# A two-layer trunk on one core: the first head unit begun on 256 tokens, and layer 1's first weights prepared between the chunks of h

## The chip, the cores and the metric

The kernel runs on one NeuronCore of a Trainium2 chip. The engines are TensorE (PE, with its weight loads shown apart as PEld), VectorE (DVE), ScalarE (ACT), GpSimd (POOL) and SyncE (SP), each with its own instruction queue; they meet only at semaphores. The metric is the device time of one execution in microseconds (us).

## The reference, cut to what matters

Two layers over 512 tokens of width 1024. Layer 0 has sliding attention with sinks, layer 1 has differential attention; each is followed by a gated feed-forward block of width 2816 with a three-tap convolution.

```python
def rms_norm(x, gain):
    y = xf * lax.rsqrt(jnp.mean(xf * xf, axis=-1, keepdims=True) + NORM_EPS)
    return (y * gain).astype(x.dtype)
...
for i in range(DEPTH):                      # DEPTH = 2
    h = rms_norm(x, attn_norm[i])
    y = sliding_sink_attention(h, ...) if kind == 0 else differential_attention(h, ...)
    x = x + y
    x = x + conv_ffn(rms_norm(x, ffn_norm[i]), ffn_w_up[i], ffn_conv_w[i], ffn_conv_b[i], ffn_w_down[i])
return rms_norm(x, final_norm)
...
q, k, v = split(h @ w_in)                   # q and k then turned by cos and sin of the positions
a = silu(conv(h @ w_up_a) + conv_b) * (h @ w_up_gate);  y = a @ w_down
```

## The kernel before

Every float32 product is made of three passes on TensorE in a 32-bit format of reduced precision: an operand is split in a high part (`w_hi`, `h_hi`, a rounded copy that ScalarE makes) and a low part (`w_lo`, `h_lo`, the difference, which VectorE makes; GpSimd made it for the first two weight blocks). So a weight block goes by DMA to `raw`, by ScalarE to `w_hi`, by VectorE to `w_lo`, and only then may TensorE use it. `raw`, `w_hi` and `w_lo` have two slots of 3072 columns. Blocks of the attention are cut in four parts of 768 columns (two chunks of 128 input features each); blocks of the down projection fill only the first 1024 columns of a slot, which are parts 0 and 1 of what follows in it.

The activations `xT` (features on partitions, tokens along the row) are eight chunks `kc` of 128 features x 512 tokens. `h = xT * gain` is split chunk by chunk: ScalarE writes `h_hi` (L1031), VectorE `h_lo` (L1383). The factor of the mean square is applied later, when a projection's tile is taken out of PSUM (`take`, L1055 to L1060).

**The start.** SP issues the loads in order: positions, the first gain, the four 128-token tiles of x (512 KB each), the first weight block in two halves of three DMAs, the second block, the small vectors. TensorE turns x with 32 transposes (L545), tile by tile. VectorE works out the angles of the rotation, copies each chunk from PSUM (L1504) and subtracts (L1383); ScalarE takes the four sines, the squares of two tiles, and then alternates between `h_hi` and a part of `w_hi`. GpSimd subtracts the eight parts of the first two blocks (L518). TensorE's first projection (L594) is the head unit 0: two token tiles side by side chunk by chunk (48 products of 384 columns), then the other two tiles (48 more), then the first tile of unit 1 (24), then the head transposes of unit 0 (L608). These need the rotated q and k: `take` of all four tiles by ScalarE, then `rope` on VectorE (L1395 to L1400), and the vectors copied by `little_vectors` (L1512 to L1519).

**The end of the down projection of layer 0.** The last pair of blocks is ordered so that the eight output chunks end one after the other: with 16 groups of three products, chunks 0 to 3 end with groups 4, 6, 8 and 10, chunks 4 to 7 with groups 12 to 15 (counted from 0). VectorE adds each to `xT` (L1628) and subtracts for `h_lo`; ScalarE writes `h_hi`. The first unit of layer 1 needs the parts of its weight block in slot 0: parts 2 and 3 can be split as soon as they have landed, parts 0 and 1 only when block 20 of the down projection has been read, which is after group 11. The semaphore `lo_done` counts parts in the order 2, 3, 0, 1. TensorE's first product there waits for part 0, that is for the third count, and for chunk 0 of `h_lo`. The program order of ScalarE and VectorE is written out by hand in each engine's block.

## Time and profile before

| | us |
|---|---|
| median of three runs | 1174.99 (1174.76 to 1175.63) |
| the profiled execution, its own time | 1174.54 |
| its span in the trace | 1172.8 |
| TensorE busy | 1140.1 (97%) |
| VectorE busy | 688.9 (59%) |
| ScalarE busy | 462.2 (39%) |
| GpSimd busy | 19.0 (2%) |

The trace covers 1172.8 us of the 1174.54; the other 1.7 us lie around it. In the timeline, an instruction's listed time reaches some 0.08 us into the next one's on VectorE and ScalarE, and about 0.16 us on TensorE for 384 columns, since instructions are pipelined. What an engine needs per instruction is the distance between two starts.

### The profile page before, as it was taken

The page shows a single profiled execution, that of the slowest core. Times are in us where ns is not written, and L with a number is a line of the kernel's source. Part 1 is how long each engine was busy: PE and PEld are TensorE (multiplying, and loading weights), DVE is VectorE, ACT ScalarE, POOL GpSimd, SP SyncE. Part 2 cuts the span into 40 slices and gives each one's busy share as a digit, 9 for nine tenths or more (in the row PEclk, how much of TensorE's full clock was granted, in tenths as well). Part 3 has the DMA queues.
Part 4 walks back from the last instruction along what each step waited for, and adds up shares of the span by engine and source line. Part 5 has one row for each costly group of instructions (what it writes and reads, how often), then busy time and mean ns, then how long its engine had stood idle before and what let it go on. Part 6 is the DMA issues. An engine that isn't in the chain of part 4 may idle for free.

```text
span 1172.8 us, 15982 instructions
## 1 busy us (share of the span) xinstructions
PE 1140.1 (97%) x5752; PEld 966.2 (82%) x5752; DVE 688.9 (59%) x1153; ACT 462.2 (39%) x939; POOL 19.0 (2%) x36
## 2 busy tenths in 40 slices
PE   7999899999999999998999999999999999999997
PEld 6998688888888878887999988778888888888886
DVE  5588765565565553337577777855556556553334
ACT  6577653122122222336455556554212212222324
POOL 4100000000000000000000000000000000000000
PEclk8999999999999999999999999999999999999999
DMA  7211223323323222325112311214332332213222
GB/s 225 72 37 37 73 88 92 96 84 107 105 74 107 72 72 94 102 89 162 55 54 69 94 36 36 72 40 122 108 92 86 107 103 76 89 54 105 92 91 106
DMA packets 146603, 101.94 MB, mean 87 GB/s; under 512 B 12073, under 2 KB 139270, under 8 KB 146566
## 3 DMA queue, kind: packets, MB, share of 16 engines
q1 hardware_dynamic: 146566, 101.45, 28.1%
q8 instruction: 23, 0.38, 0.1%
q14 instruction: 14, 0.11, 0.0%
HBM read 99.34 MB, written 2.10 MB: 86 GB/s over the span
## 4 chain that ended last, share of the span: by engine, by line
PE 87%; DVE 7%; ACT 4%; issue 1%; DMA 1%; SPq 0%; DVEq 0%; ACTq 0%
PE ps L529 22%; PE ps L531 22%; PE ps L530 21%; PE ps L594 15%; PE ps L608 2%; PE ps L746 2%; ACT prob L1091 1%; DVE w_lo L1354 1%; DVE h_lo L1383 1%; PE ps L772 1%; PE ps L818 1%; DVE ot_lo L1563 1%; ACT w_hi L1014 1%; ACT prob L1101 1%; DVE den L1441 0%
## 5 line engine op out<-in xcount | busy, mean ns | idle before, releaser
L1014 ACT ACTIVATE w_hi<-raw 128x512 fp32r<-128x512 f32 (+2 forms) x212 | 192.5, 940 | 302.6 <-PE ps L531 299.7
L529 PE MATMUL ps<-h_hi,w_lo 128*128 128x512 f32 x704 | 274.7, 390 | 0.0
L531 PE MATMUL ps<-h_hi,w_hi 128*128 128x512 f32 x704 | 273.9, 389 | 0.0
L530 PE MATMUL ps<-h_lo,w_hi 128*128 128x512 f32 x704 | 273.9, 389 | 0.0
L1354 DVE TENSOR_TENSOR w_lo<-raw,w_hi 128x512 fp32r<-128x512 f32 (+2 forms) x204 | 215.6, 1082 | 6.2 <-ACT w_hi L1014 6.2
L530 PEld LDWEIGHTS ps<-h_lo,w_hi 128*128 128x128 f32 x704 | 132.1, 188 | 27.9 <-issue 0.5
L529 PEld LDWEIGHTS ps<-h_hi,w_lo 128*128 128x128 f32 x704 | 132.1, 188 | 27.7 <-issue 0.5
L531 PEld LDWEIGHTS ps<-h_hi,w_hi 128*128 128x128 f32 x704 | 132.1, 188 | 27.6
L594 PE MATMUL ps<-w_hi,h_lo 128*128 128x384 f32 x384 | 133.4, 347 | 8.6 <-DVE w_lo L1354 4.5
L594 PE MATMUL ps<-w_hi,h_hi 128*128 128x384 f32 x384 | 133.2, 347 | 0.0
L594 PE MATMUL ps<-w_lo,h_hi 128*128 128x384 f32 x384 | 132.5, 345 | 0.0
L1657 DVE TENSOR_TENSOR normed<-ps,rstd 128x512 f32<-128x512 f32 x44 | 30.4, 692 | 173.1 <-PE ps L531 160.3
L1648 DVE TENSOR_TENSOR u_lo<-u_all,u_hi 128x512 fp32r<-128x512 f32 x44 | 30.4, 692 | 139.9 <-ACT u_hi L1216 139.9
L1216 ACT ACTIVATE u_hi<-u_all 128x512 fp32r (+1 forms) x44 | 27.7, 630 | 149.6 <-PE ps L531 149.6
L594 PEld LDWEIGHTS ps<-w_hi,h_lo 128*128 128x128 f32 x384 | 73.6, 192 | 13.0 <-issue 5.6
L594 PEld LDWEIGHTS ps<-w_lo,h_hi 128*128 128x128 f32 x384 | 73.5, 191 | 0.7
L594 PEld LDWEIGHTS ps<-w_hi,h_hi 128*128 128x128 f32 x384 | 73.4, 191 | 0.4
L529 PE MATMUL ps<-u_hi,w_lo 128*128 128x512 f32 x176 | 68.7, 390 | 0.6 <-DVE u_all L1666 0.3
L529 PE MATMUL ps<-w_hi,u_lo 128*128 128x512 f32 x176 | 68.8, 391 | 0.2 <-DVE w_lo L1354 0.2
L531 PE MATMUL ps<-u_hi,w_hi 128*128 128x512 f32 x176 | 68.5, 389 | 0.0
L530 PE MATMUL ps<-u_lo,w_hi 128*128 128x512 f32 x176 | 68.5, 389 | 0.0
L531 PE MATMUL ps<-w_hi,u_hi 128*128 128x512 f32 x176 | 68.5, 389 | 0.0
(188 smaller groups left out, 1583.2 us busy)
## 6 DMA issues: line engine op xcount, KB each, us to landing
raw<-in_ffn_w_up SPq DMA_DIRECT2D x88, 512.0 KB, 4.5
raw<-in_ffn_w_down SPq DMA_DIRECT2D x44, 512.0 KB, 3.3
raw<-in_b_w_in SPq DMA_DIRECT2D x24, 512.0 KB, 4.9
raw<-in_a_w_out SPq DMA_DIRECT2D x4, 1024.0 KB, 4.9
raw<-in_b_w_out SPq DMA_DIRECT2D x4, 1024.0 KB, 4.7
raw<-in_a_w_in SPq DMA_DIRECT2D x3, 1024.0 KB, 5.8
x_tok<-in_x SPq DMA_DIRECT2D x4, 512.0 KB, 4.8
out<-x_tok SPq DMA_DIRECT2D x8, 256.0 KB, 2.0
```

What stands on the lines that cost most here:

```text
L529: pe.matmul(out_, a_lo, b_hi, start=start, stop=False)
L530: pe.matmul(out_, a_hi, b_lo, start=False, stop=False)
L531: return pe.matmul(out_, a_hi, b_hi, start=False, stop=stop)
L594: ins = pe.matmul(ps[:, pj(u, t), 0:UW], a[:, kc, tok], b[:, kc, :], start=(kc == 0 and m == 0), stop=(kc == KC - 1 and m == 2))
L608: ins = pe.transpose(ps[:, bank, c * P:(c + 1) * P], i, ident[:, :])
L746: pe.matmul(ps[:, s_bank(t) + e, 0:n], a[rows, 0, q], b[rows, 1, 0:n], start=(m == 0), stop=False)
L772: ins = pe.matmul(both, v[:, s, k, :], pt[:, :, k * P:(k + 1) * P], start=(i == 0), stop=(i == len(passes) - 1))
L1014: act.activation(w_hi[:, s, at], raw[:, s, at], ACT.Copy).then_inc(hi_done, 1)
L1216: act.activation(u_hi[:, s, :], u_all[:, bass.ds(f, 1), :], ACT.Copy).then_inc(uhi_done, 1)
L1354: dve.tensor_tensor(w_lo[:, s, at], raw[:, s, at], w_hi[:, s, at].bitcast(F32), ALU.subtract).then_inc(lo_done, 1)
L1648: dve.tensor_tensor(u_lo[:, s, :], u_all[:, bass.ds(f, 1), :].rearrange("p a b -> p (a b)"), u_hi[:, s, :].bitcast(F32), ALU.subtract).the ...
L1657: own.link(dve.tensor_tensor(a, ps[:, 2 * s, :], rstd[:, :], ALU.mult))
```

## The change

At the start:

- SP loads two tiles of x, both halves of the first weight block, and then the other two tiles. The positions and the gain are loaded from ScalarE's queue. ScalarE loads the table with the sines at once and the other one later.
- TensorE runs 12 transposes of the identity that nobody reads (`keep_running`), then turns two tiles, then 32 more unread transposes, then the new `first_pair`: the projection of tiles 0 and 1, and after each of its chunks 3 to 6 four transposes of tiles 2 and 3. The projection of tiles 2 and 3 then goes chunk by chunk over both.
- Copies, `h_hi` and `h_lo` of unit 0's h are made in halves of 256 tokens.
- GpSimd subtracts no weights. VectorE subtracts the first block's parts between the halves of h, and the second block's after two tiles of v.
- The angles, the squares and the sines come after the first half of h and the first block's weights.

At the end of layer 0's down projection, ScalarE makes a part of `w_hi` after each of the first four chunks of `h_hi`, in the order 2, 3, 0, 1, where parts 2 and 3 came ahead of all chunks and 0 and 1 after the fourth and fifth. VectorE subtracts a part after each of the chunks 0 to 3 of `h_lo`, where 2 and 3 came ahead of all of its additions and 0 and 1 after chunks 4 and 5.

```diff
-            for t in range(NT):
+            for t in range(2):
                 sp.dma_start(x_tok[:, t, :], xv[:, t, :]).then_inc(x_landed[t], 16)
...
+            for t in range(2, NT):
+                sp.dma_start(x_tok[:, t, :], xv[:, t, :]).then_inc(x_landed[t], 16)
...
+            def keep_running(k):
+
+
+                for _ in range(k):
+                    pe.transpose(ps[:, 3, 0:P], ident[:, :], ident[:, :])
+
+            keep_running(12)
...
+            for t in range(2):
                 pe.wait_ge(x_landed[t], 16)
...
+                    ins = pe.transpose(first_x(kc, t), x_tok[:, t, kc * P:(kc + 1) * P], ident[:, :])
+                    if t == 1:
+                        ins.then_inc(x_tr0, 1)
+            keep_running(32)
...
+            def first_pair():
+
+
+                wh = w_hi[:, 0, :].rearrange("p (k n) -> p k n", k=KC)
+                wl = w_lo[:, 0, :].rearrange("p (k n) -> p k n", k=KC)
+                pe.wait_ge(posT_done, 2)
+                for kc in range(KC):
+                    if kc % 2 == 0:
+                        pe.wait_ge(lo_done, part_done("attnA", 0, kc // 2))
+                    pe.wait_ge(hlo_done0, kc + 1)
+                    for t in range(2):
+                        tok = slice(t * P, (t + 1) * P)
+                        ins = hi_lo(ps[:, t, 0:UW], h_hi[:, kc, tok], h_lo[:, kc, tok],
+                                    wh[:, kc, :], wl[:, kc, :], start=(kc == 0), stop=(kc == KC - 1))
+                        if kc == KC - 1:
+                            ins.then_inc(proj_done, 1)
+                    if kc >= FIRST_BACK:
+                        for t in range(2, NT):
+                            pe.wait_ge(x_landed[t], 16)
+                        for k in (2 * (kc - FIRST_BACK), 2 * (kc - FIRST_BACK) + 1):
+                            if k >= KC:
+                                continue
+                            pe.wait_ge(x_ready0, k // 2 * 2 + 2)
+                            for t in range(2, NT):
+                                ins = pe.transpose(first_x(k, t), x_tok[:, t, k * P:(k + 1) * P], ident[:, :])
+                            ins.then_inc(x_tr, 1)
...
+            act.dma_start(pos_i[:, :], positions.rearrange("b (t p) -> (b t) p", p=P))\
+               .then_inc(pos_landed, 16)
+            act.dma_start(grow[:, :], attn_norm[0].rearrange("(k p) -> k p", p=P))\
+               .then_inc(gain_landed, 16)
+            act.preload_act_table_set("trig_and_small")
...
+            for kc in range(0, KC, 2):
+                gained0(0, kc)
+                gained0(0, kc + 1)
+                high0(kc // 2)
+            for t in range(NT):
+                square_tokens(t)
+            trigonometry()
+            for kc in range(4):
+                gained0(1, kc)
+            act.preload_act_table_set("natural_log_exp_and_others")
             act.wait_ge(const_done, CONSTS)
             act.wait_ge(x_sq, NT)
             rsqrt(NORM["A"], rstd_tok[:, :], x_ss[:, :], 1.0 / D)
-
-
-            high("attnA", 1, 0, None, 0)
-            for t in range(NT):
+            for kc in range(4, KC):
+                gained0(1, kc)
+                if kc % 2:
+                    take("A", 0, 0, kc // 2 - 2)
+            for c in range(4):
+                high("attnA", 1, 0, None, c, wait=(c == 0))
+            for t in range(2, NT):
                 take("A", 0, 0, t)
-                if t < NT - 1:
...
-                high("attnB", 0, 0, None, 2, wait=True)
-                high("attnB", 0, 0, None, 3)
                 for dc in range(KC):
                     gained(NORM["B"], dc, vecT[:, 1, R_ATTN + dc:R_ATTN + dc + 1])
-                    if 3 <= dc < 5:
-                        high("attnB", 0, 0, (down, FB - 2), dc - 3, wait=False)
+                    if dc < 2:
+                        high("attnB", 0, 0, None, 2 + dc, wait=(dc == 0))
+                    elif dc < 4:
+                        high("attnB", 0, 0, (down, FB - 2), dc - 2, wait=False)
...
+            for kc in range(4):
+                copy_x(0, kc)
+            for kc in range(0, KC, 2):
+                low_h0(0, kc)
+                low_h0(0, kc + 1)
+                low_w("attnA", 0, 0, kc // 2)
+                if kc < 4:
+                    copy_x(0, kc + 4)
+                    copy_x(0, kc + 5)
+            angles()
+            copy_x(1, 0)
+            copy_x(1, 1)
+            for kc in range(KC):
+                low_h0(1, kc)
+                if kc + 2 < KC:
+                    copy_x(1, kc + 2)
...
+                    for c in range(4 if kind == "A" and t == 1 else 0):
+                        low_w("attnA", 1, 1, c)
...
-                    if 5 <= dc < 7:
-                        low_w("attnB", 0, 0, dc - 5)
+                    if 1 <= dc < 5:
+                        low_w("attnB", 0, 0, (dc + 1) % 4)
 
                 if l == 0:
-                    low_w("attnB", 0, 0, 2)
-                    low_w("attnB", 0, 0, 3)
```

TensorE at the start of the program, before (`x_tok` holds x by token tiles, `ps` is PSUM; `lo_done` counts weight parts, `hlo_done` chunks of h):

```order
L545 MATMUL ps<-ident,x_tok 128x128 [waits x_landed0]
L545 MATMUL ps<-ident,x_tok 128x128 x5
L545 MATMUL ps<-ident,x_tok 128x128 [waits posT_done]
L545 MATMUL ps<-ident,x_tok 128x128
L545 MATMUL ps<-ident,x_tok 128x128 [waits x_landed1]
L545 MATMUL ps<-ident,x_tok 128x128 x7
L545 MATMUL ps<-ident,x_tok 128x128 [waits x_landed2]
L545 MATMUL ps<-ident,x_tok 128x128 x7
L545 MATMUL ps<-ident,x_tok 128x128 [waits x_landed3]
L545 MATMUL ps<-ident,x_tok 128x128 x7
L594 MATMUL ps<-w_hi,h_lo 128x384 [waits hlo_done,lo_done,const_done]
```

and in the changed kernel:

```order
L538 MATMUL ps<-ident 128x128 [waits ident_done]
L538 MATMUL ps<-ident 128x128 x11
L542 MATMUL ps<-ident,pos_f 128x4 [waits pos_done]
L544 MATMUL ps<-ident,grow 128x8 [waits gain_landed]
L549 MATMUL ps<-ident,x_tok 128x128 [waits x_landed0]
L549 MATMUL ps<-ident,x_tok 128x128 x7
L549 MATMUL ps<-ident,x_tok 128x128 [waits x_landed1]
L549 MATMUL ps<-ident,x_tok 128x128 x7
L538 MATMUL ps<-ident 128x128 x32
L528 MATMUL ps<-w_hi,h_lo 128x384 [waits lo_done,hlo_done0,posT_done,const_done]
L529 MATMUL ps<-w_lo,h_hi 128x384
L530 MATMUL ps<-w_hi,h_hi 128x384
```

The first projection moved from behind four tiles' transposes to behind those of two and 44 unread ones.

VectorE at the end of layer 0's down projection, before:

```order
L1354 TENSOR_TENSOR w_lo<-raw,w_hi 128x768 [waits hi_done] x2
L1628 TENSOR_TENSOR xT<-xT,ps 128x512 [waits down_done] x2
L1383 SCALAR_TENSOR_TENSOR h_lo<-xT,vecs,h_hi 128x512 [waits hhi_done]
L1628 TENSOR_TENSOR xT<-xT,ps 128x512 [waits down_done]
L1383 SCALAR_TENSOR_TENSOR h_lo<-xT,vecs,h_hi 128x512 [waits hhi_done]
L1628 TENSOR_TENSOR xT<-xT,ps 128x512 [waits down_done]
L1383 SCALAR_TENSOR_TENSOR h_lo<-xT,vecs,h_hi 128x512 [waits hhi_done]
L1628 TENSOR_TENSOR xT<-xT,ps 128x512 [waits down_done]
L1383 SCALAR_TENSOR_TENSOR h_lo<-xT,vecs,h_hi 128x512 [waits hhi_done]
L1628 TENSOR_TENSOR xT<-xT,ps 128x512 [waits down_done]
L1383 SCALAR_TENSOR_TENSOR h_lo<-xT,vecs,h_hi 128x512 [waits hhi_done]
L1354 TENSOR_TENSOR w_lo<-raw,w_hi 128x768 [waits hi_done]
```

and in the changed kernel:

```order
L1712 TENSOR_TENSOR xT<-xT,ps 128x512 [waits down_done] x2
L1441 SCALAR_TENSOR_TENSOR h_lo<-xT,vecs,h_hi 128x512 [waits hhi_done]
L1412 TENSOR_TENSOR w_lo<-raw,w_hi 128x768 [waits hi_done]
L1712 TENSOR_TENSOR xT<-xT,ps 128x512 [waits down_done]
L1441 SCALAR_TENSOR_TENSOR h_lo<-xT,vecs,h_hi 128x512 [waits hhi_done]
L1412 TENSOR_TENSOR w_lo<-raw,w_hi 128x768 [waits hi_done]
L1712 TENSOR_TENSOR xT<-xT,ps 128x512 [waits down_done]
L1441 SCALAR_TENSOR_TENSOR h_lo<-xT,vecs,h_hi 128x512 [waits hhi_done]
L1412 TENSOR_TENSOR w_lo<-raw,w_hi 128x768 [waits hi_done]
L1712 TENSOR_TENSOR xT<-xT,ps 128x512 [waits down_done]
L1441 SCALAR_TENSOR_TENSOR h_lo<-xT,vecs,h_hi 128x512 [waits hhi_done]
L1412 TENSOR_TENSOR w_lo<-raw,w_hi 128x768 [waits hi_done]
```

The first additions moved ahead of the first two weight parts, and the last two parts moved up among chunks 2 and 3.

ScalarE at the same place, before:

```order
L1014 ACTIVATE w_hi<-raw 128x768 [waits raw_landed0]
L1014 ACTIVATE w_hi<-raw 128x768
L1031 ACTIVATE h_hi<-xT,vecs 128x512 [waits x_ready] x4
L1014 ACTIVATE w_hi<-raw 128x768 [waits down_used]
L1031 ACTIVATE h_hi<-xT,vecs 128x512 [waits x_ready]
L1014 ACTIVATE w_hi<-raw 128x768
L1031 ACTIVATE h_hi<-xT,vecs 128x512 [waits x_ready] x3
```

and in the changed kernel:

```order
L1067 ACTIVATE h_hi<-xT,vecs 128x512 [waits x_ready]
L1050 ACTIVATE w_hi<-raw 128x768 [waits raw_landed0]
L1067 ACTIVATE h_hi<-xT,vecs 128x512 [waits x_ready]
L1050 ACTIVATE w_hi<-raw 128x768
L1067 ACTIVATE h_hi<-xT,vecs 128x512 [waits x_ready]
L1050 ACTIVATE w_hi<-raw 128x768 [waits down_used]
L1067 ACTIVATE h_hi<-xT,vecs 128x512 [waits x_ready]
L1050 ACTIVATE w_hi<-raw 128x768
L1067 ACTIVATE h_hi<-xT,vecs 128x512 [waits x_ready] x4
```

Each part of `w_hi` now follows a chunk of `h_hi`; the wait for the landed block stands behind the first chunk.

## Rows read from the trace of the kernel before

**Rows 1.** The page, part 1: engine, busy us (share), instructions.
```profile
PE 1140.1 (97%) x5752; PEld 966.2 (82%) x5752; DVE 688.9 (59%) x1153; ACT 462.2 (39%) x939; POOL 19.0 (2%) x36
```

**Rows 2.** To 19.4 us: length, busy PE, PEld, DVE, ACT, POOL; PEclk; DMA share; GB/s.
```profile
4.80:10.80 6.00, 5.91 (x32) 5.68 (x32) 1.24 (x6) 4.17 (x9) 0.00 (x0) 1.00 1.06 364
10.80:14.40 3.60, 0.00 (x0) 0.01 (x1) 3.60 (x5) 3.57 (x6) 1.96 (x2) 0.78 1.13 356
14.40:19.40 5.00, 4.98 (x16) 5.00 (x17) 5.00 (x6) 3.25 (x5) 5.00 (x3) 0.50 0.83 227
```

**Rows 3.** Waits of 0 to 48 us: total, times, longest us.
```profile
PE ps L594 <- POOL w_lo L518: 3.7, 1, 3.7
```

**Rows 4.** Groups of instructions, 8 to 28 us: busy us, mean ns, idle before.
```profile
L518 POOL TENSOR_TENSOR w_lo<-raw,w_hi 128x768 fp32r<-128x768 f32 x5 | 10.5, 2116 | 13.8 <-ACT w_hi L1014 13.8
L1383 DVE SCALAR_TENSOR_TENSOR h_lo<-xT,vecs,h_hi 128x512 fp32r<-128x512 f32 x8 | 9.7, 1229 | 0.0
...
L1031 ACT ACTIVATE h_hi<-xT,vecs 128x512 fp32r<-128x512 f32 x8 | 5.7, 715 | 5.0 <-DVE xT L1504 5.0
L1504 DVE COPY xT<-ps 128x512 f32<-128x512 f32 x8 | 5.3, 681 | 4.7 <-PE ps L545 4.7
L1014 ACT ACTIVATE w_hi<-raw 128x768 fp32r<-128x768 f32 x6 | 5.0, 832 | 0.0
...
L1119 ACT ACTIVATE sq<-x_tok 128x1024 f32<-128x1024 f32 x4 | 4.2, 1055 | 0.2
```

**Rows 5.** TensorE at the end of the first down projection.
```profile
540.10 0.39 PE L531 MATMUL ps<-u_hi,w_hi 128*128 128x512 f32 x1
544.97 0.45 PE L594 MATMUL ps<-w_hi,h_lo 128*128 128x384 f32 x1 [4.48 <-DVE w_lo L1354]
```

**Rows 6.** VectorE there.
```profile
535.03 1.83 DVE L1354 TENSOR_TENSOR w_lo<-raw,w_hi 128x768 fp32r<-128x768 f32 x2 [2.55 <-ACT w_hi L1014]
536.78 1.28 DVE L1628 TENSOR_TENSOR xT<-xT,ps 128x512 f32<-128x512 f32 x2
...
543.97 0.95 DVE L1354 TENSOR_TENSOR w_lo<-raw,w_hi 128x768 fp32r<-128x768 f32 x1
```

**Rows 7.** ScalarE there.
```profile
534.16 1.58 ACT L1014 ACTIVATE w_hi<-raw 128x768 fp32r<-128x768 f32 x2 [2.67 <-DMA raw<-in_b_w_in]
...
557.13 1.28 ACT L1252 ACT_TABLE_LOAD   x1
```

**Rows 8.** Busy time by stretch at that place, columns as in rows 2.
```profile
545.00:550.00 5.00, 5.00 (x20) 5.00 (x21) 4.77 (x8) 2.94 (x5) 0.00 (x0) 0.66 0.29 84
```

**Rows 9.** The chain that ended last, from 540 us.
```profile
544.97 15.71 PE ps L594 x80
...
561.47 7.04 PE ps L594 x40
```

**Rows 10.** The same helper where GpSimd is quiet, 527 to 549 us, columns as in rows 4.
```profile
L1383 DVE SCALAR_TENSOR_TENSOR h_lo<-xT,vecs,h_hi 128x512 fp32r<-128x512 f32 x8 | 6.0, 746 | 0.3 <-ACT h_hi L1031 0.2
```

**Rows 11.** DMA issues begun near 3.35 us: KB, us from issue to landing.
```profile
x_tok<-in_x SPq DMA_DIRECT2D x1, 512.0 KB, 6.2
raw<-in_a_w_in SPq DMA_DIRECT2D x1, 512.0 KB, 7.0
```

**Rows 12.** Weight loads of the x transposes, first 4.8 to 8.3 us.
```profile
L545 PEld LDWEIGHTS ps<-ident,x_tok 128*128 128x128 f32 x17 | 3.5, 224 | 1.9 <-DMA x_tok<-in_x 1.9
```

**Rows 13.** The same weight loads, 9 to 11 us.
```profile
L545 PEld LDWEIGHTS ps<-ident,x_tok 128*128 128x128 f32 x12 | 1.6, 156 | 0.0
```

**Rows 14.** TensorE, the first head transposes after the first unit.
```profile
38.87 1.47 PE L608 MATMUL ps<-ident,qk 128*128 128x128 f32 x12
```

**Rows 15.** VectorE, the last step before those transposes.
```profile
3.82 0.64 DVE L1490 SCALAR_TENSOR_TENSOR ang<-turns,ang 128x32 f32<-128x32 f32 x3
...
37.98 0.36 DVE L1519 TENSOR_SCALAR nsink<-sink_in 64x16 f32<-64x16 f32 x2
```

**Rows 16.** ScalarE, end of the first head unit: start us, us.
```profile
34.69 0.31 ACT L1055 ACTIVATE qk<-ps,vecs 128x64 f32<-128x64 f32 x1 [2.44 <-PE ps L594]
```

More of the change, by code:

```diff
@@ L44 @@
 UA, UB = 4, 8
+FIRST_BACK = 3
 OB, ODC = 4, 2
@@ L66 @@
 CONSTS = 1 + HALF + 4 + 10
-FIRST_LOWS = 2
 ALU = mybir.AluOpType
@@ L510, in _ @@
             pool.wait_ge(const_done, CONSTS)
-            def low(ph, s, i):
-                n = cols(ph) // parts(ph)
-                for c in range(parts(ph)):
-                    at = slice(c * n, (c + 1) * n)
-                    pool.wait_ge(hi_done, part_done(ph, i, c))
-                    pool.tensor_tensor(w_lo[:, s, at], raw[:, s, at], w_hi[:, s, at].bitcast(F32),
-                                       ALU.subtract).then_inc(lo_done, 1)
-            for i in range(FIRST_LOWS):
-                low("attnA", i, i)
         @block.tensor
@@ L622, in start_unit0 @@
             def start_unit0(kind):
-                slabs = chain(projection(kind, 0, 0, (0, 1)), projection(kind, 0, 0, (2, 3)))
-                run(slabs, 12 + 8)
+                if kind == "A":
+                    first_pair()
+                    slabs = projection(kind, 0, 0, (2, 3))
+                    run(slabs, 8)
+                else:
+                    slabs = chain(projection(kind, 0, 0, (0, 1)), projection(kind, 0, 0, (2, 3)))
+                    run(slabs, 12 + 8)
                 if kind == "B":
@@ L1120, in square_tokens, with gained0, high0 @@
                                accum_out=x_ss[:, t:t + 1]).then_inc(x_sq, 1)
-            square_tokens(0)
-            square_tokens(1)
-            for kc in range(KC):
-                gained(NORM["A"], kc, vecT[:, 0, R_ATTN + kc:R_ATTN + kc + 1])
-                if kc == 0:
-                    act.wait_ge(half_landed, 16 * 3)
-                if kc < 4:
-                    high("attnA", 0, 0, None, kc, wait=(kc == 2))
-            square_tokens(2)
-            square_tokens(3)
+            def gained0(pair, kc):
+                act.wait_ge(x_ready if pair else x_ready0, kc + 1)
+                at = pair_cols(pair)
+                act.activation(h_hi[:, kc, at], xT[:, kc, at], ACT.Copy,
+                               scale=vecT[:, 0, R_ATTN + kc:R_ATTN + kc + 1])\
+                   .then_inc(hhi_done if pair else hhi_done0, 1)
+            def high0(c):
+                if c == 0:
+                    act.wait_ge(half_landed, 16 * 3)
+                high("attnA", 0, 0, None, c, wait=(c == 2))
+            for kc in range(0, KC, 2):
[8 more added lines that the diff above has]
+            act.preload_act_table_set("natural_log_exp_and_others")
             act.wait_ge(const_done, CONSTS)
@@ new lines, in copy_x, with low_h0 @@
+            def copy_x(pair, kc):
+                dve.wait_ge(x_tr if pair else x_tr0, kc // 2 * 2 + 2)
+                dve.tensor_copy(xT[:, kc, pair_cols(pair)], first_x(kc)).then_inc(x_ready if pair else x_ready0, 1)
+            def low_h0(pair, kc):
+                dve.wait_ge(hhi_done if pair else hhi_done0, kc + 1)
+                at = pair_cols(pair)
+                dve.scalar_tensor_tensor(out=h_lo[:, kc, at], in0=xT[:, kc, at],
+                                         scalar=vecT[:, 0, R_ATTN + kc:R_ATTN + kc + 1],
+                                         in1=h_hi[:, kc, at].bitcast(F32), op0=ALU.mult,
+                                         op1=ALU.subtract).then_inc(hlo_done if pair else hlo_done0, 1)
```

84 lines of the change are left out of this document (38 added, 46 removed).

## The prediction

> **What bounds the kernel now.** The page comes first: TensorE is busy for 97% of the span [rows 1], so only its gaps and its slow stretches can be won, and the change touches two. The stretches of the start show 3.6 us without a product between the last transpose of x and the first product, and behind them 5.0 us with 16 products at granted clock 0.50, the 1.2 GHz level [rows 2]. The waits name what ended that gap: the first low part of the weights, from GpSimd [rows 3]. The groups say why all this is slow: GpSimd needs 2,116 ns for a part, and VectorE's `h_lo`, which reads two SBUF tensors, has a mean of 1,229 ns beside it [rows 4], while copies of the same size from PSUM take 681 ns [rows 4]. The second place is the end of layer 0's down projection. TensorE starts its last product there at 540.10 and the next at 544.97, waiting 4.48 us for a low part on VectorE [rows 5]. VectorE did not make its first addition until 536.78, because two weight parts stood ahead of it and were waiting for a transfer that ended at 534.16 [rows 6, 7]. The granted clock then is 0.66 over 545 to 550 us [rows 8], and the first 80 products take 15.71 us, where 40 others take 7.04, or 0.175 each [rows 9].
>
> **Durations used.** Start to start, VectorE's instruction is about 0.08 us shorter than listed (two additions in 1.28, each listed near 0.68 [rows 6]); likewise on ScalarE. For 256 columns there is no row. Bounds are half of the 512-column pitch and the whole of it: 0.30 to 0.60 for a copy, 0.33 to 0.66 for `h_lo` (its pitch is 0.66, from 746 ns where GpSimd is quiet [rows 10]), 0.31 to 0.63 for `h_hi` [rows 4]. I take 0.34, 0.39 and 0.42, near the half, since 768 columns against 512 on ScalarE cost 832 against 715 ns [rows 4], which leaves a fixed part of some 0.2 to 0.4. A weight part costs ScalarE 0.75 and VectorE 0.87 [rows 4, 6].
>
> **The start, part by part.**
>
> *Loads.* Positions and gain leave SP's queue, so x starts about 0.8 us sooner; a tile of x needs 1.4 us of the transfer engines (the first had landed at 4.85, the fourth, issued near 2.9, 6.2 later [rows 2, 11]). Two tiles then land at about 4.1 and 5.3. The first weight half landed at 10.4 to 11.4 [rows 11]; with two tiles fewer ahead I put it at 7.7. The second half follows at 10.5, and tiles 2 and 3, now behind both, at 13.8 instead of 9.1. The second block and the small vectors are needed later than they land.
>
> *TensorE up to the first product.* The weight loads of the x transposes took 224 ns at first and 156 on average from 9 us on [rows 12, 13], although the granted clock reads 1.00 all through [rows 2]: the engine began at 1.2 GHz and rose after some 4.5 us of transposes alone. Twelve unread transposes from 1.5 us cost 2.5 us at that level. They cover nothing but the wait for x (4.1), so they cost at most 0.2. If the clock rises 4.5 us after that, at 6.0, the transposes of x end at 7.0 and the 32 unread ones (0.11 each, as in rows 14, where twelve take some 1.3) at 10.5. The page "TensorE: Matmul & The Clock Gate" of the Trainium skill, section "Part 4: PE-mode transpose", says that full clock "doesn't engage" for transposes, which do not count as busy in the same way. By that rule the unread transposes would only delay; rows 12 and 13 contradict it here, and it is the second rival below.
>
> *The first weights.* VectorE copies four halves of chunks from 6.6 on; ScalarE has two `h_hi` at 7.9 and `w_hi` at 8.6; VectorE has the two `h_lo` by then and the part at 9.6. That is before the unread transposes end, so the first product starts at 10.5, against 14.42 before (where rows 2 change). The later parts come at 11.9, 14.2 and 15.9, and TensorE needs them at 12.6, 15.1 and 18.1: nothing waits. The first pair is 48 products at 0.175 plus 16 transposes at 0.11, together 10.2 us, to 20.7.
>
> *The second pair.* VectorE does the angles (ten small operations at 0.21 [rows 15], 2.1 us) and two copies until 18.8. ScalarE is later: four squares at 1.24 from 14.0 to 19.0 (1,055 ns [rows 4] and a read of the sum), sines 0.5, then `h_hi`. Its first chunk of the second half is ready at 20.5, just under TensorE's 20.7. ScalarE then loads a table (1.28 [rows 7]) and makes the reciprocal root, done at 23.9; chunk 4 is ready at 24.9 and TensorE wants it at 24.9. So 48 products end at 29.2.
>
> *The chain behind it.* TensorE adds 24 products and two transposes of vectors and would reach the head transposes at 33.8. ScalarE does not let it: from 23.9, four `h_hi` (1.7), two takes at 0.95, four parts of the second block (3.0), so takes 2 and 3 begin at 30.5, and the last one at 31.4. Before, from the last take's start to the head transposes' inputs it was 34.69 to 38.3 at most [rows 15, 16], of which 3.4 is work. So they start at 31.4 + 3.4 + latency = 34.9. Before they started at 38.87 [rows 14]. **Gain 3.9 us**, and TensorE idles about 1.1 us at that point, which is what is late next. GpSimd's parts and the slow `h_lo` go at no cost: VectorE has 8 x 0.87 more, and its idle time above covers it.
>
> **The end of the down projection.** TensorE's groups last 0.68 us (three products) and the last begins its third product at 540.10 [rows 5]. So chunk 0 is done at 533.0, chunks 1 to 3 at 534.4, 535.7 and 537.1, and block 20 has been read at 537.8. VectorE was free from 532.5. In the new order VectorE adds chunk 0 at 533.0 and ScalarE has `h_hi` 0 at 534.4, when the transfer has just ended [rows 7]. Then the two engines alternate: additions 0.60, `h_lo` 0.66, parts 0.87 on VectorE. Part 2 is done at 536.6, part 3 at 538.7, part 0 (its `w_hi` started at 537.9, just after block 20 was read) at 540.9, part 1 at 543.0. Before, part 0 started at 543.97 [rows 6]. The first product comes at 540.9 instead of 544.97: 4.05 us. TensorE reaches chunk 2 at 543.0, when part 1 is there; every later chunk (2.13 us of VectorE for two at 1.26, against 2.1 on TensorE) is ready before it. With a gap of 0.6 us the clock stays up: 80 products take 14.0 instead of 15.71, 1.7 more.
>
> What could eat it: the squares' end moves only 1.6 us forward, and four parts and the table load follow. The load started at 557.13 [rows 7]; it now starts at 555.6 and ends at 556.9, where the mean square is there at 555.7. The takes are thus 1.3 us late against a slack of 1.6 before the head transposes, and unit 1's first product waits perhaps 0.1. **Gain 5.7 us.**
>
> **Sum.** 3.9 + 5.7 = 9.6 us. Against the profiled execution's own 1174.54 that is 1164.9; the median of the runs lies 0.45 above that execution, so I predict **1165.4 us**. The stretches in between are a stream on TensorE that is not touched.
>
> **Rivals.**
>
> 1. *Two helpers too slow at the start.* If halves cost nearer their upper bound, some 20% more on VectorE, the schedule above ends at 37.8 instead of 34.9. For: both queues have many short waits on each other, and small instructions have fixed costs. Against: rows 4 and 6. Time: 1.1 + 5.7 gained, 1168.2.
> 2. *Transposes don't hold the clock.* TensorE stays at 1.2 GHz: the 32 unread ones then take 7 us and the first product starts at 14.5, with the clock rising some 5 us later. Head transposes at 40.0, 1.1 late. Only the second place gains: 1174.99 + 1.1 - 5.7 = 1170.4. Against it stand rows 12 and 13.
> 3. *The second place gains only in part*, say because the weight transfer lands later or the clock falls all the same: 2.2 us less, 1167.6.
> 4. *Slower.* The transfer of x tiles 2 and 3 is the mechanism: the first pair's chunk 3 is followed by a wait for both, in TensorE's own order, with the rest of the first pair queued behind. From a landing at 15.2 on each microsecond costs one; the start stops winning at 20.2 and the whole kernel loses from about 25.9. At 28 it would be 1177. Against: 2.6 MB stand ahead, at 356 to 364 GB/s [rows 2] some 7 us.
> 5. *It does nothing*, because TensorE's later waits give both gains back: 1175.
>
> **Chances.** Forecast 60%, rival 1 17%, rival 3 10%, rival 2 8%, rival 4 2%, rival 5 3%. Lower bound: no lateness of ScalarE (33.8, 5.1 gained), first product a little sooner and 5.8 at the second place, or 1163.3. The upper end takes in rivals 1 and 3: 1168.6. About 0.2% (2.35 us) is what a measurement of this kernel can tell from no change. Forecast and rivals 1 to 3 lie beyond that: faster 95%, same 3%, slower 2%.
>
> **What would show it.** Right: the first projection product near 10.5 us at full clock; no GpSimd work after 5 us; the head transposes near 34.9, released by VectorE; no gap above 1 us before layer 1's first product (near 537, since all there comes 3.9 sooner) and no half clock after it. Wrong: a clock of 0.50 between 10 and 20 us; a wait of TensorE for x tiles; a wait for the low part at the second place over 1.5 us.

## The result and the profile after

| | before | after |
|---|---|---|
| median of the runs, us | 1175.05 (1174.76 to 1175.63) | 1165.69 (1165.55 to 1165.93) |
| span of the profiled execution, us | 1172.8 | 1163.7 |

The ratio is 0.9918, with a 95% interval of 0.9904 to 0.9932. The changed kernel is 9.4 us faster; the prediction was 1165.4 us, in a range from 1163.3 to 1168.6. Timed once more (e8 below) it was 10.7 us faster by the medians, mostly because the kernel before was slower there (1175.8). The two ratios have overlapping intervals, and the account below, which follows one trace of each kernel, explains 9.1 us.

The page of the changed kernel, part 1 (engine, busy us, share, instructions), answers to [rows 1]:

```profile
PE 1141.4 (98%) x5796; PEld 966.4 (83%) x5796; DVE 693.7 (60%) x1177; ACT 464.8 (40%) x947; POOL 3.0 (0%) x28
```

TensorE has 44 instructions more (the unread transposes) and the span is 9.1 us shorter. GpSimd has lost 16 us of work, VectorE has gained only 4.8 us of busy time although it took over eight weight parts: its own `h_lo` became faster.

**The start, TensorE.** The timeline of the changed kernel (start us, length us, line, operation, tiles, count, idle time and its releaser):

```profile
1.53 2.82 PE L538 MATMUL ps<-ident 128*128 128x128 f32 x12 [1.53 <-POOL ident L505]
...
4.59 2.85 PE L549 MATMUL ps<-ident,x_tok 128*128 128x128 f32 x16
7.28 3.66 PE L538 MATMUL ps<-ident 128*128 128x128 f32 x32
10.72 0.41 PE L528 MATMUL ps<-w_hi,h_lo 128*128 128x384 f32 x1
```

The first product starts at 10.72, without a wait, where it started at 14.42 before. Products then follow each other by 0.175 us; before, the first 16 took 5 us at granted clock 0.50 [rows 2]. The window of 10 to 15 us, which answers to [rows 2], is full at granted clock 1.00 (columns: length; busy us of PE, PEld, DVE, ACT, POOL; PEclk; DMA share; GB/s):

```profile
10.00:15.00 5.00, 5.00 (x33) 4.89 (x32) 5.00 (x11) 4.40 (x9) 0.00 (x0) 1.00 1.04 382
```

**The start, the helpers.** Groups of instructions over the first 28 us (busy us, mean ns, idle before) and two rows of the timelines, which answer to [rows 4]:

```profile
L1170 ACT ACTIVATE h_hi<-xT,vecs 128x256 fp32r<-128x256 f32 x16 | 7.4, 503 | 5.7 <-DVE xT L1564 5.7
L1569 DVE SCALAR_TENSOR_TENSOR h_lo<-xT,vecs,h_hi 128x256 fp32r<-128x256 f32 x16 | 7.3, 480 | 2.5 <-ACT h_hi L1170 2.4
```

```profile
6.90 1.42 DVE L1564 COPY xT<-ps 128x256 f32<-128x256 f32 x4 [2.03 <-PE ps L549]
...
8.62 0.85 ACT L1050 ACTIVATE w_hi<-raw 128x768 fp32r<-128x768 f32 x1 [0.35 <-DMA raw<-in_a_w_in]
```

**The head transposes.** They start at 35.00 instead of 38.87 [rows 14], behind VectorE, and this is now the only wait that the view of waits lists for TensorE between 5 and 40 us (total us, times, longest us):

```profile
PE ps L639 <- DVE vecs L1597: 0.7, 1, 0.7
```

**The end of the down projection.** TensorE's last product there and the first of layer 1 answer to [rows 5]:

```profile
536.40 0.39 PE L530 MATMUL ps<-u_hi,w_hi 128*128 128x512 f32 x1
537.23 0.44 PE L598 MATMUL ps<-w_hi,h_lo 128*128 128x384 f32 x1 [0.45 <-DVE w_lo L1412]
```

From start to start that is 0.83 us instead of 4.87. The chain of work that ended last, from there on, answers to [rows 9]:

```profile
534.18 0.87 DVE w_lo L1412
535.05 0.60 DVE xT L1712
535.65 0.66 DVE h_lo L1441
536.31 0.88 DVE w_lo L1412
537.19 0.04 issue
537.23 14.19 PE ps L598 x80
551.42 0.79 PE ps L571 x8
552.20 7.15 PE ps L598 x40
559.35 0.87 PE ps L639 x8
```

The 80 products take 14.19 us instead of 15.71. Ahead of them the chain runs over VectorE alone (addition, `h_lo`, low part, 2.13 us a round): VectorE still ends last there, by under half a microsecond.

**Where 9.1 us went.** 3.87 at the head transposes; 0.17 of it is lost again up to the last product of the down projection (536.40 against 540.10, or 3.70); 4.04 in the gap; 1.52 in the 80 products; minus 0.11 in the next 40. That makes 9.15 us at layer 1's head transposes (559.35 against 568.51 in the chain before), and the span is 9.1 shorter.

### The profile page after: what moved, and what is told of

The parts are those of the page before. It is cut to its first block, busy times and chain, and to the rows that moved or that the text cites. A ratio compares the mean times of both kernels' runs of the same rounds, so it can differ in the third digit from the quotient of the medians.

```text
span 1163.7 us, 16099 instructions
## 1 busy us (share of the span) xinstructions
PE 1141.4 (98%) x5796; PEld 966.4 (83%) x5796; DVE 693.7 (60%) x1177; ACT 464.8 (40%) x947; POOL 3.0 (0%) x28
## 4 chain that ended last, share of the span: by engine, by line
PE 87%; DVE 6%; ACT 5%; issue 1%; DMA 1%; SPq 0%; DVEq 0%; ACTq 0%
PE ps L528 22%; PE ps L530 22%; PE ps L529 22%; PE ps L598 14%; PE ps L639 2%; PE ps L782 2%; ACT prob L1127 1%; DVE w_lo L1412 1%; PE ps L808 1%; ACT w_hi L1050 1%; PE ps L854 1%; DVE ot_lo L1648 1%; DMA raw<-in_a_w_in 1%; ACT prob L1137 1%; DVE den L1499 0%
## 5 line engine op out<-in xcount | busy, mean ns | idle before, releaser
L1412 DVE TENSOR_TENSOR w_lo<-raw,w_hi 128x512 fp32r<-128x512 f32 (+2 forms) x212 | 223.1, 1077 | 4.4 <-ACT w_hi L1050 4.4
L598 PE MATMUL ps<-w_hi,h_lo 128*128 128x384 f32 x368 | 126.5, 344 | 0.4 <-DVE w_lo L1412 0.4
L598 PE MATMUL ps<-w_hi,h_hi 128*128 128x384 f32 x368 | 126.2, 343 | 0.0
L598 PE MATMUL ps<-w_lo,h_hi 128*128 128x384 f32 x368 | 125.5, 341 | 0.0
L598 PEld LDWEIGHTS ps<-w_hi,h_lo 128*128 128x128 f32 x368 | 69.2, 188 | 5.0 <-issue 2.1
L598 PEld LDWEIGHTS ps<-w_lo,h_hi 128*128 128x128 f32 x368 | 69.2, 188 | 0.7
L598 PEld LDWEIGHTS ps<-w_hi,h_hi 128*128 128x128 f32 x368 | 69.2, 188 | 0.4
L529 PE MATMUL ps<-w_lo,u_hi 128*128 128x512 f32 x176 | 68.5, 389 | 0.0
```

Source lines behind the costliest of these rows:

```text
L529: pe.matmul(out_, a_hi, b_lo, start=False, stop=False)
L598: ins = pe.matmul(ps[:, pj(u, t), 0:UW], a[:, kc, tok], b[:, kc, :], start=(kc == 0 and m == 0), stop=(kc == KC - 1 and m == 2))
L1412: dve.tensor_tensor(w_lo[:, s, at], raw[:, s, at], w_hi[:, s, at].bitcast(F32), ALU.subtract).then_inc(lo_done, 1)
```

## Experiments

The theory: two gains that add, one at each place. At the start it is the first product that comes earlier and at full clock, and the head transposes are then held up by ScalarE's chain and not by TensorE. GpSimd's parts are slow themselves and slow VectorE down. At the second place, the order on VectorE and ScalarE. The rivals are those of the prediction. "Head" below is the start of the first head transposes, "layer 1" the start of its first product, both from the profile. Every kernel was timed beside the kernel before, whose median was 1176.05 next to e1 to e4, 1175.8 next to e5 to e8 and 1175.66 next to e9 and e10.

| kernel | head | layer 1 | median us | ratio, 95% interval |
|---|---|---|---|---|
| before | 38.87 | 544.97 | 1175.05 | |
| changed | 35.00 | 537.23 | 1165.69 | 0.9918 (0.9904 to 0.9932) |
| e8, changed again | 34.51 | 536.68 | 1165.12 | 0.9910 (0.9896 to 0.9923) |
| e1, second place alone | 39.45 | 542.11 | 1169.9 | 0.9946 (0.9933 to 0.9960) |
| e2, start alone | 34.31 | 540.50 | 1170.12 | 0.9954 (0.9941 to 0.9968) |
| e3, no unread transposes | 35.59 | 537.65 | 1165.4 | 0.9910 (0.9895 to 0.9925) |
| e4, before with 38 unread | 38.81 | 545.13 | 1173.58 | 0.9981 (0.9972 to 0.9990) |
| e5, early angles | 35.29 | 537.30 | 1164.92 | 0.9904 (0.9889 to 0.9919) |
| e6, e5 without unread | 35.66 | 538.24 | 1164.52 | 0.9902 (0.9887 to 0.9917) |
| e7, GpSimd's parts back | 38.23 | 540.34 | 1169.25 | 0.9942 (0.9929 to 0.9956) |
| e9, e5 with 22 unread | 33.91 | 536.00 | 1164.15 | 0.9901 (0.9887 to 0.9915) |
| e10, x tiles 2 and 3 late | 38.72 | 541.24 | 1168.75 | 0.9939 (0.9926 to 0.9952) |

In the kernels with the new second place, layer 1 starts 502.0 to 502.7 us after the head transposes, whatever happened ahead of them: what is won or lost at the start arrives there within 0.7 us.

e8 is the changed kernel, unedited, beside e5 to e7. It was expected 9.4 us under the kernel before, with the head transposes at 35.0 and a ratio within 0.3 us of the first one. It came 10.7 us under by the medians, with the head transposes at 34.51 and a ratio that is 0.9 us lower, so comparisons of two kernels to within 1 us need their traces too.

### e1 and e2: each place alone

e1 is the kernel before with only this:

```diff
-                high("attnB", 0, 0, None, 2, wait=True)
-                high("attnB", 0, 0, None, 3)
...
-                    if 3 <= dc < 5:
-                        high("attnB", 0, 0, (down, FB - 2), dc - 3, wait=False)
+                    if dc < 2:
+                        high("attnB", 0, 0, None, 2 + dc, wait=(dc == 0))
+                    elif dc < 4:
+                        high("attnB", 0, 0, (down, FB - 2), dc - 2, wait=False)
...
-                    if 5 <= dc < 7:
-                        low_w("attnB", 0, 0, dc - 5)
+                    if 1 <= dc < 5:
+                        low_w("attnB", 0, 0, (dc + 1) % 4)
...
-                    low_w("attnB", 0, 0, 2)
-                    low_w("attnB", 0, 0, 3)
```

> The kernel before with only the second edit: at the end of layer 0's down projection, ScalarE's and VectorE's weight parts between the chunks of h. My theory (the two places add, and the second is worth 4.0 us of gap and 1.5 us of clock): 5.5 us less than before, 1169.5 us, ratio 0.9953. Rival (the gain of the changed kernel comes from the start, and the second gap would come back later): less than 2 us.

e2 is the changed kernel with these lines undone.

> The changed kernel with the second edit undone, so only the start is new. My theory: 3.7 to 3.9 us less than before, 1171.2 us, ratio 0.9967; with e1 the two gains add up to that of both. Rival (an overlap between the two): the gains of e1 and e2 add up to more or less than the whole by over 1 us.

Measured: 1169.9 and 1170.12 against 1176.05, or 6.2 and 5.9 us less by the medians (5.4 by the ratio of e2). Both are more than expected: 5.5 for e1, 3.7 to 3.9 for e2. The chain of e1 shows the whole gain of the second place without the start:

```profile
542.06 0.04 issue
542.11 14.19 PE ps L594 x80
556.29 0.79 PE ps L567 x8
557.08 7.16 PE ps L594 x40
```

The chain of e2 shows the old second place under the new start:

```profile
540.50 15.71 PE ps L598 x80
556.21 0.79 PE ps L571 x8
556.99 7.04 PE ps L598 x40
```

The spans are 4.4 and 4.5 us shorter than before; in e1 the untouched start came 0.58 later than in the trace of before (39.45), so its own part is 5.0. 5.0 and 4.5 make 9.5, where both together gave 9.1: by the traces the gains add within 0.4 us. The medians alone don't show it: they add up to 12.1 against 9.4 for the changed kernel and 10.7 for e8. That is over the 1 us that the rival asked for, but each ratio is known only to about 1.6 us. What stands is that in e1 the 80 products and the gap before them are those of the changed kernel (14.19, and 0.84 from 541.27), and that in e2 they are those of the kernel before (15.71, and 4.87 from 535.63).

### e3: without the unread transposes

```diff
-            keep_running(12)
...
-            keep_running(32)
```

> The changed kernel without any of the 44 unread transposes. Theory A (they hold the clock, and ScalarE's chain hides most of that): the first products run at half clock for 2 to 5 us, but the head transposes wait for ScalarE and VectorE anyway, so 0 to 0.7 us more than the changed kernel. Theory B (the clock is what wins the start): 2 to 3 us more. The Trainium skill's page TensorE: Matmul & The Clock Gate, Part 4, says transposes do not count as busy; by it nothing would change in the clock, and the first product would start no later than now.

Measured: 1165.4, ratio 0.9910, the same as the changed kernel in e8. The clock does fall. TensorE in e3:

```profile
4.67 3.29 PE L548 MATMUL ps<-ident,x_tok 128*128 128x128 f32 x16
11.25 0.66 PE L528 MATMUL ps<-w_hi,h_lo 128*128 128x384 f32 x1 [3.29 <-DVE w_lo L1410]
11.71 0.52 PE L529 MATMUL ps<-w_lo,h_hi 128*128 128x384 f32 x1
...
14.44 0.34 PE L529 MATMUL ps<-w_lo,h_hi 128*128 128x384 f32 x1
...
35.59 1.47 PE L637 MATMUL ps<-ident,qk 128*128 128x128 f32 x12
```

Nine products cost 0.32 instead of 0.175 until 14.26, and the granted clock of 10 to 15 us is 0.66. That makes 1.3 us, and 0.5 more for a first product at 11.25. But the head transposes come only 0.59 later than in the changed kernel and wait for nobody: ScalarE's lateness had covered the rest. The account closes. From the first product to the head transposes TensorE needs 22.98 and 23.00 us in e5 and e9 below, where it neither waits nor slows down; it takes 24.28 in the changed kernel and 24.19 in e8, so the helpers hold it up by 1.2 to 1.3 us there, and 24.34 in e3, where the slow products fill the same 1.3 us. Without the unread transposes the clock fell, so the last sentence of the expectation did not come true.

### e4: unread transposes in the gap of the kernel before

```diff
+                if kind == "B":
+                    pe.wait_ge(x_ready, KC * NORM["B"] + 1)
+                    for _ in range(38):
+                        pe.transpose(ps[:, 0, 0:P], ident[:, :], ident[:, :])
```

> The kernel before with nothing but 38 unread transposes of the identity (about 4.2 us at full clock) put into the 4.5 us gap ahead of layer 1's first product. If transposes hold the clock, the granted clock stays 1.00 over 545 to 550 us and the first 80 products take 14.1 us instead of 15.71: 1.5 us less than before, 1173.5 us. If transposes do not count, the clock falls as before and the time is that of before, within 0.3 us.

Measured: 1173.58, ratio 0.9981 (0.9972 to 0.9990), so 1.2 to 3.3 us less; the expected 1.5 lies within, and the spans differ by 1.4. TensorE at that place, the piece of the chain, and the window that answers to [rows 8] (same columns, granted clock 1.00 for 0.66):

```profile
540.32 4.31 PE L628 MATMUL ps<-ident 128*128 128x128 f32 x38
545.13 0.45 PE L594 MATMUL ps<-w_hi,h_lo 128*128 128x384 f32 x1 [0.50 <-DVE w_lo L1358]
```

```profile
545.13 14.20 PE ps L594 x80
```

```profile
545.00:550.00 5.00, 4.87 (x28) 4.80 (x29) 4.77 (x9) 2.77 (x5) 0.00 (x0) 1.00 0.27 78
```

The gap before the product is as long as before, but it is filled with transposes, and the 80 products take 14.20 instead of 15.71 [rows 9]. So transposes alone keep the engine at 2.4 GHz. The page "TensorE: Matmul & The Clock Gate" of the Trainium skill, section "Part 4: PE-mode transpose", says the full clock doesn't engage for transpose mode, next to figures for bf16; for the float32 transposes of this kernel these rows contradict that. The run also splits the second place's gain: 1.5 us are the clock and the other 4.0 the gap itself.

### e5, e6 and e9: the helpers' work put into their idle time

In the changed kernel ScalarE waits 4.4 us for the first copy of x, while it later works out four squares and the sines in a row. e5 puts the angles, the first two squares and the sines there:

```diff
+            square_tokens(0)
+            square_tokens(1)
+            trigonometry()
             for kc in range(0, KC, 2):
...
-            for t in range(NT):
+            for t in range(2, NT):
                 square_tokens(t)
-            trigonometry()
...
+            angles()
             for kc in range(4):
                 copy_x(0, kc)
```

> The changed kernel with its ScalarE and VectorE work for the start put into the idle time before the first h_hi: VectorE works out the ten small steps of the angles from 4.8 us, ahead of the copies of x, and ScalarE squares tiles 0 and 1 and makes the sines ahead of the first h_hi. Nothing is left out. Theory A (the helpers' chain, not TensorE, sets when the head transposes start in the changed kernel, 35.00 against 34.0 at which TensorE is ready): ScalarE's work behind the first pair shrinks by 3 us, the takes of tiles 2 and 3 start with the end of their products near 29.7, head transposes at 34.2, total 0.8 us under the changed kernel of the same call. Rival B: the first h_hi moves from 7.36 to 8.5 or later because the square of tile 1 has to wait for its tile, the first product comes 0.5 to 1 us later, and nothing is gained: within 0.3 us of the changed kernel.

e6 is e5 without the 12 and 32 unread transposes.

> The kernel of e5_early_angles without the 12 and the 32 unread transposes, nothing else. Theory A (the unread transposes are worth about 1.6 us on TensorE, which in the changed kernel lies under ScalarE's lateness): with the helpers early nothing hides the slow products any more; the first nine or ten products run at the 1.2 GHz pitch of 0.32, head transposes near 35.6 and total 1.4 us above e5. Rival B (what e3 showed holds whatever the helpers do): within 0.4 us of e5.

Measured: 1164.92 and 1164.52, so e5 is 0.2 us under e8 and e6 0.4 under e5. In both the size is that of rival B and not that of theory A, but mostly for another reason than rival B's. ScalarE was early enough (the take of tile 2 begins after 2.0 us of idle time at 30.59 in e5; in e8 it begins at 30.20 straight behind the weight parts), but TensorE was later. TensorE in e5:

```profile
5.05 3.68 PE L549 MATMUL ps<-ident,x_tok 128*128 128x128 f32 x16
...
12.31 0.42 PE L528 MATMUL ps<-w_hi,h_lo 128*128 128x384 f32 x1
...
35.29 1.47 PE L639 MATMUL ps<-ident,qk 128*128 128x128 f32 x12
```

All 16 transposes of x ran at the 1.2 GHz pace (0.22 each), so the 32 unread ones ended at 12.3, when VectorE's low part had been there since 10.9. In e6 it is the products that pay:

```profile
11.10 0.41 PE L528 MATMUL ps<-w_hi,h_lo 128*128 128x384 f32 x1 [2.99 <-DVE w_lo L1412]
...
12.25 0.52 PE L528 MATMUL ps<-w_hi,h_lo 128*128 128x384 f32 x1
...
15.71 0.34 PE L530 MATMUL ps<-w_hi,h_hi 128*128 128x384 f32 x1
```

The window of 12 to 16 us of e6 has granted clock 0.57, that of 11 to 12 still 1.00:

```profile
12.00:16.00 4.00, 4.00 (x16) 4.00 (x15) 4.00 (x9) 3.39 (x6) 0.00 (x0) 0.57 1.06 357
```

The clock falls at 12.2, although the first product found it high, and 11 products cost 0.315: 1.5 us. In e5 the unread transposes cost 1.4 us of waiting for their own end. The two kernels differ by 0.4 us in total time, which their runs don't tell apart. The profiled execution of e6 was its slowest (1166.35, the others 1164.47 to 1164.57), so the slow products need not be in the others.

The explanation was that 32 are too many for an engine that is at 1.2 GHz when they begin. e9 has 22:

```diff
-            keep_running(32)
+            keep_running(22)
```

> The kernel of e5_early_angles with 22 instead of 32 unread transposes behind those of x, nothing else. In e5 the first low part was ready at 10.9 and TensorE reached the first product only at 12.31, because the transposes ran at the 1.2 GHz pitch until about 9.3 us. Theory A (the length of the row of unread transposes sets the first product there, and its clock is kept by a gap under 0.5 us): first product 11.1 to 11.5 at 0.17 to 0.18 pitch, head transposes at 34.4, which no helper holds up, total 0.9 us under e5, so 0.9896 of the kernel before. Rival B (with fewer of them the clock falls for part of the first pair, as in e6): 9 or more products at the 0.32 pitch, head transposes at 35.3 to 35.8, total within 0.5 us of e5.

Measured: 1164.15 (1164.07 to 1164.27), 0.8 us under e5 by the medians (expected 0.9; the head transposes came at 33.91, expected at 34.4). The best run of e5, 1164.04, is as fast: its runs lie from there to 1165.56, and the profiled one, with the late clock, was 1165.37. If the clock rises early, 32 transposes end in time too, so what 22 gain is probably the executions in which it rises late. That is my reading of the spread; no trace shows an execution of e5 with an early clock. TensorE in e9:

```profile
8.44 2.72 PE L538 MATMUL ps<-ident 128*128 128x128 f32 x22
10.91 0.42 PE L528 MATMUL ps<-w_hi,h_lo 128*128 128x384 f32 x1
...
33.91 1.47 PE L639 MATMUL ps<-ident,qk 128*128 128x128 f32 x12
```

No wait stands at the head transposes and no product is slow. e9 is the fastest of all kernels run: 1.0 to 1.5 us under the two measurements of the changed kernel, whose runs (1164.76 to 1166.13) don't overlap with its own. The ratios to the kernel before, 0.9901 against 0.9910 and 0.9918, have overlapping intervals, so the gain rests on the runs' own spread and on the trace, not on a comparison side by side.

### e7: the first low parts on GpSimd again

```diff
+            def low(ph, s, i):
...
+                    pool.tensor_tensor(w_lo[:, s, at], raw[:, s, at], w_hi[:, s, at].bitcast(F32),
+                                       ALU.subtract).then_inc(lo_done, 1)
+
+            for i in range(2):
+                low("attnA", i, i)
...
-                low_w("attnA", 0, 0, kc // 2)
...
-                    for c in range(4 if kind == "A" and t == 1 else 0):
-                        low_w("attnA", 1, 1, c)
```

> The changed kernel with the low parts of the first two weight blocks back on GpSimd, as before the change; VectorE no longer makes them. Nothing is left out. Theory A (GpSimd's parts are slow, 2.1 us each, and make VectorE's h_lo slow too, listed near 0.85 to 1.0 each instead of 0.48): first product at 11.9 instead of 10.7, further waits at chunks 2, 4 and 6, head transposes near 37, total 1.5 to 2.5 us above the changed kernel. Rival B (VectorE is freed of 8 x 0.87 us and that makes up for it; GpSimd's part is no slower beside VectorE): h_lo stays at 0.48 and the total is at most 0.7 above.

Measured: 1169.25, 4.1 us above e8, and the head transposes at 38.23, 3.7 later. The direction was as expected, the size was taken too small, and the waits stand elsewhere: none at the chunks 2, 4 and 6. VectorE beside GpSimd, in e7:

```profile
8.67 0.74 DVE L1576 COPY xT<-ps 128x256 f32<-128x256 f32 x2
9.33 3.78 DVE L1581 SCALAR_TENSOR_TENSOR h_lo<-xT,vecs,h_hi 128x256 fp32r<-128x256 f32 x2
...
33.36 1.66 DVE L1465 TENSOR_TENSOR htmp<-qk,cos 128x384 f32<-128x384 f32 x1
```

GpSimd in e7:

```profile
9.02 5.80 POOL L529 TENSOR_TENSOR w_lo<-raw,w_hi 128x768 fp32r<-128x768 f32 x3 [4.84 <-ACT w_hi L1062]
...
29.18 7.52 POOL L529 TENSOR_TENSOR w_lo<-raw,w_hi 128x768 fp32r<-128x768 f32 x4 [11.97 <-ACT w_hi L1062]
```

An `h_lo` of 256 columns costs 1.89 us there, as long as one part of GpSimd (1.93), and 0.48 in the changed kernel. The copies from PSUM between them keep their 0.37. The rotation's product of the same form takes 1.66 instead of 0.55. So each of VectorE's operations with two SBUF inputs that meets one of GpSimd's lasts about as long as that one, whatever its size. That is what the Trainium skill states on the page "SBUF — State Buffer", section "SBUF: two separate sides": the port pair that both engines share is held for a whole instruction, and the other engine blocks. But most of the 3.7 us is not this slowing. TensorE's waits in e7 between 5 and 40 us are mostly on GpSimd's parts:

```profile
PE ps L610 <- POOL w_lo L529: 2.2, 4, 0.8
PE ps L540 <- POOL w_lo L529: 0.5, 1, 0.5
```

and the last of these waits in TensorE's timeline:

```profile
36.75 0.44 PE L610 MATMUL ps<-w_hi,h_lo 128*128 128x384 f32 x1 [0.77 <-POOL w_lo L529]
```

The first product comes 0.8 us later than in e8 (11.12 against 10.32). Nearly all the rest is lost at unit 1's first tile, where TensorE needs 1.05 us for the products of a part and GpSimd about 1.8 to make one, even while VectorE is idle from 28.7 to 32.2. TensorE takes the four parts up at 31.15, 32.85, 34.65 and 36.75, each time behind a wait for GpSimd. The slowed rotation on VectorE ends at about the same time (38.1) and adds a last wait of 0.17.

### e10: x tiles 2 and 3 behind the second weight block

```diff
-            for t in range(2, NT):
-                sp.dma_start(x_tok[:, t, :], xv[:, t, :]).then_inc(x_landed[t], 16)
             load("attnA", 1, 0, None)
+            for t in range(2, NT):
+                sp.dma_start(x_tok[:, t, :], xv[:, t, :]).then_inc(x_landed[t], 16)
```

> The changed kernel with the loads of x tiles 2 and 3 put behind those of the second weight block on SP's queue (1.57 MB, some 4.2 us at 370 GB/s); nothing is left out. Theory A (the prediction's fourth rival, with its price: from a landing at 15.2 us on each microsecond costs one): the tiles land near 18, TensorE waits about 3 us behind the first pair's chunk 3, part of the products behind it runs at 1.2 GHz, head transposes at 38 to 39.5 and total 3 to 4.5 us above the changed kernel. Rival B (ScalarE's lateness of 0.6 us and the slack of the squares hide part of it, or the transfer is quicker than that): total at most 1.5 us above.

Measured: 1168.75 (runs from 1166.69 to 1171.01), 3.6 us above e8; the head transposes come at 38.72. TensorE and ScalarE in e10:

```profile
18.39 1.09 PE L630 MATMUL ps<-ident,x_tok 128*128 128x128 f32 x4 [3.52 <-issue]
...
19.60 0.52 PE L529 MATMUL ps<-w_lo,h_hi 128*128 128x384 f32 x1
```

```profile
18.32 1.06 ACT L1162 ACTIVATE sq<-x_tok 128x1024 f32<-128x1024 f32 x1 [0.22 <-DMA x_tok<-in_x]
```

The wait is put down to "issue", but ScalarE's square of tile 3 shows the landing at 18.3. Until 21.8 TensorE is at 1.2 GHz (granted clock 0.57 from 18 to 22 us), which costs another 1.6 us. TensorE begins these transposes 3.7 us behind the pace of its products, so it loses 5.3 in all, and 1.2 to 1.3 of that lies under ScalarE's lateness. Theory A came, and the fourth rival's mechanism is real. Its price was too low: a landing 3.1 us behind its 15.2 costs 3.7 to 4.2 at the head transposes, and the half clock that follows the wait was not in it.

## Why the prediction was right

| step | predicted, us | measured, us |
|---|---|---|
| first product | 10.5 | 10.72 |
| second pair begins | 20.7 | 21.13 |
| products of unit 1 begin | 29.2 | 29.72 |
| head transposes | 34.9 | 35.00 |
| gain there | 3.9 | 3.87 |
| gap before layer 1, gained | 4.05 | 4.04 |
| its 80 products | 14.0 | 14.19 |
| behind them, lost | 0.1 | 0.11 |
| total | 9.6 | 9.15 in the trace, 9.4 by the medians |

**The durations** for 256 columns were near the half of those for 512, as chosen: four copies in 1.42 (0.335 each from start to start; 0.34 taken), two `h_lo` in 0.87 (0.40; 0.39 taken), two `h_hi` in 0.91 (0.41; 0.42 taken). That is why rival 1 didn't come.

**The first weights** landed later than estimated: `w_hi` began at 8.62 after a wait for the transfer, where 7.7 had been put for the landing. It cost nothing, since TensorE was in its unread transposes until 10.7.

**The chain behind the second pair** came out as worked: TensorE was ready at 34.3 (33.8 forecast), so it idled 0.7 us and not the 1.1 forecast, and VectorE released it at 35.0, behind the rotation that follows the takes. The other half microsecond is lost in small holds from the start of the second pair on (23.0 us from first product to head transposes are enough, see e3). The naming of ScalarE as what is late next was right, and e9 shows it from the other side: with that work moved and the transposes shortened, the head transposes start at 33.91.

**The clock at the start** was right in its sign, but one step of it was not a fact of the engine's work. "If the clock rises 4.5 us after that, at 6.0" held by luck: from the pace of the 16 transposes of x (2.69 us from the first to the unread ones, at 0.22 or 0.114 each) it rose near 6.4 in the changed kernel, but near 4.7 in e2 (16 in 1.87) and only near 9.3 in e5, behind the same twelve transposes from 1.53 on. The head transposes of the same kernel came at 35.00 and at 34.51. The start's gain is thus 3.9 to 4.4 in the profiles, and the forecast's 3.9 had no room for that in its wording, though its range had.

**The unread transposes** were only half priced. The prediction priced their failure (rival 2) and not their absence; e3 shows that in the changed kernel they are worth nothing that can be measured, since ScalarE's chain covers the 1.3 us of slow products. The gain at the start comes from the rest: the 256 tokens, the helpers' order, and VectorE instead of GpSimd. How it splits is not shown. With GpSimd's parts back (e7) the head transposes come at 38.23, so only 0.6 of the 3.9 us over the kernel before is left. The opposite was not run: the kernel before with its low parts on VectorE and nothing else. That could be a simpler way to much of this gain, and it is the rival that stays open. The prediction entered GpSimd's parts as something that goes "at no cost"; by e7 nearly all of the start's gain depends on their going.

**The second place** was priced within 0.25 us (5.7 forecast, 5.45 measured): the order on VectorE and ScalarE gives 4.0, the clock 1.5. e4 shows the clock's part by itself, e1 both without the new start. Most of what is missing is the term of the 80 products, rounded too far down: at the 0.176 of [rows 9] they are 14.1, and the first one after the gap costs 0.1 more.

**The rest.** 0.17 us is lost between the two places, and I did not find where.

## What to carry to other kernels

An engine that has to be kept at full clock through a gap can be fed transposes that nobody reads, but count both ends: the filler must end when the awaited input comes, at the slower pace too, or it becomes the wait. Before giving the second engine of a shared pair a subtraction "for free", look at two things: its time per part against the time in which TensorE uses one up (1.8 against 1.05 us in e7, which is most of the loss), and the mean time of the first engine's operations with two SBUF inputs while the other runs, since that slowing stands in no wait. Where a helper's chain ends last behind a new start, moving its work into the idle time ahead brings something only once TensorE itself is early enough.

## What the runs showed of the hardware

- Float32 transposes alone hold TensorE at 2.4 GHz through a gap of 4.8 us (e4: granted clock 1.00 over 545 to 550 us, and the 80 products behind them in 14.20 instead of 15.71).
- The moment at which TensorE first rises from 1.2 GHz differs from one execution to the next by 4.6 us, with the same twelve transposes ahead of those of x (near 4.7 us in e2, 6.4 in the changed kernel, 9.3 in e5). The granted clock of the windows reads 1.00 there all the same; the pace of the transposes (0.22 or 0.114 us) tells it.
- The clock can also fall some time after a gap and not at its end: in e6 the engine stood still for 3 us, took up its products at full pace at 11.10, and ran at the half from 12.25 to 15.45. In e3 the clock fell inside a gap of the same kind: the first product, at 11.25, was slow already.
- An operation of VectorE with two SBUF inputs of 256 columns takes 1.89 us beside GpSimd's 1.93, against 0.48 alone; a copy from PSUM is not slowed (e7). GpSimd needs about 1.8 us for its 128x768 subtraction while VectorE is idle, VectorE 0.87 to 0.96 for the same.
